# A decoder step on one core: plain 8-block products in place of Strassen's 7 in the first and last part of three token groups

## The chip, the core and the metric

The program runs on one core of one Trainium2 chip. TensorE (PE) multiplies, VectorE (DVE), ScalarE (ACT) and GpSimd (POOL) do the elementwise work, SyncE (SP) issues most weight loads; each engine runs its own instructions in order and waits on semaphores for the others. The metric is device time in microseconds, the lower the better.

## The reference, cut to what matters

One layer of a hybrid decoder over 2048 prompt tokens and 64 sample tokens, in float32. The attention and convolution mixers come first; the change lies in the feed-forward part behind them:

```python
def ffn_sublayer(x, g_pre, w_up_l, w_down_l, g_post):
    h = rmsnorm(x, g_pre)
    a = jax.nn.relu(jnp.einsum('btd,df->btf', h, w_up_l))
    return x + rmsnorm(jnp.einsum('btf,fd->btd', a * a, w_down_l), g_post)
```

with `x` of 2112 x 1024, `w_up` of 1024 x 4096 and `w_down` of 4096 x 1024. The key and value caches of the samples are also copied to outputs, shifted by 8 rows.

## The kernel before

**Number format.** Every float32 operand of a matmul is split in two fp32r tiles: ACT casts it (high part), DVE or POOL subtracts the cast from the original (low part). A product is then three matmuls: high x high, high x low, low x high. A "low" below is such a subtraction, a "split" of weights is a cast and a low.

**Tiling.** The function `out_and_mlp` takes the tokens in four groups (g = 0 to 3) of 512, 512, 512 and 576, and the 4096 hidden columns in eight parts (p = 0 to 7). Part p of group g first makes 4 blocks of 128 hidden columns (`up` steps, i = 0 to 3; 8 blocks of the inner dimension x 3 = 24 matmuls of 512 columns each), ReLU and square on ACT, and then multiplies these 512 hidden columns by the 512 x 1024 block of `w_down` and adds to the group's output `mixed(g)` (tile `em_hx` for even groups, `em_y` for odd ones).

**Strassen.** The product of part p, tokens (2 halves of 256) x hidden (2 halves of 256) times hidden (2) x outputs (2 halves of 512), is done in 7 products (`down` steps in the order P1, P7, P2, P6, P5, P4, P3) instead of 8. Each is 2 token tiles x 2 blocks x 3 = 12 matmuls of 512 columns. The sums of weight blocks lie ready in HBM (`scratch_wt`); the sums of activations are made by DVE (`first_sums`, `second_sums`, `third_sum`: 4 per part), each operand is then split (7 casts on ACT, 5 lows on DVE, 2 on POOL). Two products go to a `shared` tile, which is added to the outputs once per group (`share`: 2 adds of 512 columns, 2 of 1024 in place of four more per part). PE writes products into 5 banks (`y_ps`), DVE adds each to its place (14 additions per part, `add_down`), and PE waits on `y_added` before it takes a bank again.

**Order of work.** `steps()` yields one list, which every engine goes through in the same order. The first two ups of part p + 1 (the *leads*) stand behind P7 and P6 of part p, so that PE has work while operands get ready. In the last part (p = 7) there are no leads; there the `h` steps stand between the products: PE turns the normalised tokens of the next group (8 transposes to two of three `up_ps` banks), ACT casts and DVE takes the low.

Around each unit n, ACT casts the weights of unit n + 2 (it waits for the use of unit n - 1), and DVE or POOL takes their low. DVE does P7, P6 and P3 (in part 7 only P6), POOL all others:

```python
LO_BY_DVE, LO_BY_DVE_LAST = (P7, P6, P3), (P6,)
BY_DVE, BY_POOL = (P1, P7, P2, P6, P5), (P4, P3)
```

Weights are loaded by SP in pieces of 1 MB for two ups or two products, three in flight. The work at the rim of the groups is placed by hand in the tables `POST`, `FIRST`, `ADD`, `PRE`, `SECOND` (norms and residual on the way into the feed-forward part, placed in parts 0 to 2 of group 0 and 5 to 7 of groups 1 and 2) and `END`, `SCALE`, `END_ADD`, `OUT` (final norm, residual and store of group g, placed in part 0 and the start of part 1 of group g + 1):

```python
END_ADD = (("up", 0, 3), ("up", 1, 0), ("up", 1, 0), ("down", 0, P5))
OUT = (("down", 0, P7), ("down", 0, P2), ("down", 0, P6), ("down", 0, P4))
```

`END_ADD` is POOL's `add_residual` (L1977), which waits for the load of the residual `x1` to `ml_res`; `OUT` is ACT's store of a finished tile (`store_y`, which waits for POOL's addition) and its load of the residual two tiles on (L1864). In even parts ACT also issues a copy of 3 MB of the key or value cache from HBM to HBM behind the last up (L118), on the same queue.

Lines: L2095 to L2097 are the matmuls of an up, L2171 those of a product of 7, L2128 those of the mixers' output projection, L2080 the turns of h, L2203 ACT's weight cast, L1983 and L2485 the weight lows of POOL and DVE, L2266 and L2479 cast and low of activations, L2451 their sums, L2511 and L2513 DVE's additions out of the banks, L2534 and L2538 the shares, L2562 a norm's scaling.

## Time and profile before

| what | value |
|---|---|
| time, median of 3 runs | 2646.51 us (2641.0 to 2647.37) |
| the profiled execution: time, span | 2644.41 us, 2642.6 us |
| mean granted TensorE clock | 0.984 |
| PE busy | 2522.6 us, 95% of the span |
| DVE, ACT, POOL busy | 1382.9, 1166.3, 1415.2 us |
| feed-forward parts, roughly | from 1043 us to the end |

A row of the trace names the engine, the line of the kernel, the operation, the tiles written and read with their shapes, and how many instructions it groups. In brackets stands how long the engine was idle before it and what ended that. Times of rows are microseconds from the start of the span. Matmuls overlap: one of 0.39 us starts every 0.23.

### The profile page before, as it was taken

What the parts mean: (1) busy time and instruction counts of PE and PEld (TensorE: products, weight loads), DVE (VectorE), ACT (ScalarE), POOL (GpSimd) and SP (SyncE); (2) the same over time, 40 slices, a digit from 0 to 9 for tenths busy, and PEclk for the clock granted to TensorE, in tenths of its full rate; (3) what the DMA queues carried; (4) which work ended last, traced back from release to release, by engine and by line L of the source; (5) the groups of instructions that cost most, each with busy time, mean ns of one, the idle gap of its engine ahead of it and who ended that gap; (6) DMA issues with size and microseconds to landing.
All of it is one profiled execution on the core that took longest, in us unless ns stands there. A gap on an engine that the chain in (4) does not pass through costs nothing.

```text
span 2642.6 us, 35400 instructions
## 1 busy us (share of the span) xinstructions
PE 2522.6 (95%) x13562; PEld 2167.4 (82%) x13562; DVE 1382.9 (52%) x2231; ACT 1166.3 (44%) x2002; POOL 1415.2 (54%) x818
## 2 busy tenths in 40 slices
PE   7999999999999999999998999998999999999995
PEld 6899999899996468778877788777778778889884
DVE  6431221265663225865566554676555476655657
ACT  4000110187775534545454444554544455444443
POOL 1216560068663566665566675666665475554555
PEclk9999999999999999999999999999999999999998
DMA  5316764299988944564556555456555263553452
GB/s 183 112 44 244 264 230 120 83 164 180 166 146 212 295 160 166 193 208 159 167 183 242 176 168 183 151 170 232 173 173 193 99 235 120 198 178 127 142 191 96
DMA packets 297903, 457.65 MB, mean 173 GB/s; under 512 B 81748, under 2 KB 202140, under 8 KB 290776
## 3 DMA queue, kind: packets, MB, share of 16 engines
q1 hardware_dynamic: 270546, 313.71, 41.3%
q10 hardware_dynamic: 14518, 89.43, 9.5%
q0 software_dynamic: 12672, 52.24, 5.9%
q8 instruction: 109, 1.79, 0.3%
q14 instruction: 58, 0.48, 0.1%
HBM read 390.50 MB, written 120.53 MB: 193 GB/s over the span
## 4 chain that ended last, share of the span: by engine, by line
PE 76%; DVE 10%; DMA 5%; POOL 3%; ACT 3%; issue 2%; SPq 0%; ACTq 0%; DVEq 0%; POOLq 0%
PE ml_y L2171 13%; PE ml_up L2095 8%; PE ml_up L2096 8%; PE ml_up L2097 8%; PE ml_y L2128 6%; PE pj_acc L518 6%; PE pj_acc L519 6%; PE pj_acc L520 6%; PE at_o L1187 5%; PE at_turn L1167 2%; POOL ml_w_lo L1983 2%; DVE ml_a_lo L2479 2%; DVE ml_a_lo_raw L2451 2%; DVE ml_w_lo L2485 2%; PE at_score L1156 2%
## 5 line engine op out<-in xcount | busy, mean ns | idle before, releaser
L1983 POOL TENSOR_TENSOR ml_w_lo<-em_raw,ml_w_hi 128x1024 fp32r<-128x1024 f32 x296 | 741.2, 2512 | 635.1 <-ACT ml_w_hi L2203 634.9
L2203 ACT CAST ml_w_hi<-em_raw 128x1024 fp32r<-128x1024 f32 x384 | 401.4, 1046 | 295.8 <-PE ml_y L2171 189.0
L2095 PE MATMUL ml_up<-ml_h_hi,ml_w_hi 128*128 128x512 f32 (+2 forms) x1280 | 457.1, 357 | 23.3 <-POOL ml_w_lo L1983 23.3
L2096 PE MATMUL ml_up<-ml_h_lo,ml_w_hi 128*128 128x512 f32 (+2 forms) x1280 | 453.5, 354 | 0.0
L2097 PE MATMUL ml_up<-ml_h_hi,ml_w_lo 128*128 128x512 f32 (+2 forms) x1280 | 452.6, 354 | 0.0
L2171 PE MATMUL ml_y<-ml_w_hi,ml_a_hi 128*128 128x512 f32 x896 | 358.2, 400 | 34.4 <-DVE em_hx L2513 13.8
L2171 PE MATMUL ml_y<-ml_w_lo,ml_a_hi 128*128 128x512 f32 x896 | 352.6, 393 | 0.0
L2171 PE MATMUL ml_y<-ml_w_hi,ml_a_lo 128*128 128x512 f32 x896 | 352.3, 393 | 0.0
L2095 PEld LDWEIGHTS ml_up<-ml_h_hi,ml_w_hi 128*128 128x128 f32 x1280 | 243.2, 190 | 66.3 <-POOL ml_w_lo L1983 35.3
L518 PE MATMUL pj_acc<-pj_h_hi,pj_w_hi 128*128 128x424 f32 (+1 forms) x800 | 290.3, 363 | 5.6 <-DVE pj_h_lo L736 5.6
L519 PE MATMUL pj_acc<-pj_h_lo,pj_w_hi 128*128 128x424 f32 (+1 forms) x800 | 283.5, 354 | 0.0
L520 PE MATMUL pj_acc<-pj_h_hi,pj_w_lo 128*128 128x424 f32 (+1 forms) x800 | 283.4, 354 | 0.0
L2485 DVE TENSOR_TENSOR ml_w_lo<-em_raw,ml_w_hi 128x1024 fp32r<-128x1024 f32 x88 | 132.1, 1501 | 264.7 <-ACT ml_w_hi L2203 264.4
L2096 PEld LDWEIGHTS ml_up<-ml_h_lo,ml_w_hi 128*128 128x128 f32 x1280 | 243.4, 190 | 30.7
L2097 PEld LDWEIGHTS ml_up<-ml_h_hi,ml_w_lo 128*128 128x128 f32 x1280 | 243.1, 190 | 31.0
L2171 PEld LDWEIGHTS ml_y<-ml_w_hi,ml_a_hi 128*128 128x128 f32 x896 | 170.1, 190 | 83.8 <-DVE em_hx L2513 15.7
L754 DVE SCALAR_TENSOR_TENSOR pj_proj<-pj_acc,pj_scale,pj_rstd_of 128x424 f32<-128x424 f32 (+1 forms) x100 | 65.0, 656 | 311.0 <-PE pj_acc L520 311.0
L2171 PEld LDWEIGHTS ml_y<-ml_w_hi,ml_a_lo 128*128 128x128 f32 x896 | 170.2, 190 | 36.2
L2171 PEld LDWEIGHTS ml_y<-ml_w_lo,ml_a_hi 128*128 128x128 f32 x896 | 170.5, 190 | 33.6
L2479 DVE TENSOR_TENSOR ml_a_lo<-ml_a_lo_raw,ml_a_hi 128x512 fp32r<-128x512 f32 x128 | 166.9, 1304 | 0.1
L2255 ACT ACTIVATE ml_a<-ml_up 128x512 f32<-128x512 f32 (+1 forms) x80 | 41.0, 513 | 279.4 <-PE ml_up L2097 269.6
L518 PEld LDWEIGHTS pj_acc<-pj_h_hi,pj_w_hi 128*128 128x128 f32 x800 | 150.9, 189 | 15.7 <-issue 8.3
(319 smaller groups left out, 4559.8 us busy)
## 6 DMA issues: line engine op xcount, KB each, us to landing
em_raw<-in_w_up SPq DMA_DIRECT2D x64, 1024.0 KB, 6.2
em_raw<-scratch_wt SPq DMA_DIRECT2D x128, 512.0 KB, 4.7
em_raw<-in_w_down SPq DMA_DIRECT2D x96, 512.0 KB, 3.7
out_o_a_k_s<-in_cache_a_k ACTq DMA_DIRECT2D x8, 3060.0 KB, 11.9
out_o_a_v_s<-in_cache_a_v ACTq DMA_DIRECT2D x8, 3060.0 KB, 13.2
em_raw<-scratch_pt SPq DMA_DIRECT2D x34, 512.0 KB, 7.3
pj_work<-in_w_down POOLq DMA_DIRECT2D x16, 1024.0 KB, 6.3
scratch_wt<-pj_work POOLq DMA_DIRECT2D x16, 1024.0 KB, 4.5
```

The source lines that it names most:

```text
L518: pe.matmul(acc[g][:, 0:n], w_hi[:, i % 2, k, :], h_hi[:, k, cols], start=(k == 0), stop=False)
L519: pe.matmul(acc[g][:, 0:n], w_hi[:, i % 2, k, :], h_lo[:, k, cols], start=False, stop=False)
L520: last = pe.matmul(acc[g][:, 0:n], w_lo[:, i % 2, k, :], h_hi[:, k, cols], start=False, stop=(k == DBLK - 1))
L1983: nc.gpsimd.tensor_tensor(split_of(w_lo, n), raw_of(n), f32(split_of(w_hi, n)), ALU.subtract).then_inc(w_lo_ready, 1)
L2095: pe.matmul(out, hi[:, k, :], h_hi[:, k, cols], start=(k == 0), stop=False)
L2096: pe.matmul(out, hi[:, k, :], h_lo[:, k, cols], start=False, stop=False)
L2097: last = pe.matmul(out, lo[:, k, :], h_hi[:, k, cols], start=False, stop=(k == DBLK - 1))
L2128: last = pe.matmul(out, p[:, f, t0:t0 + m], w[:, b, :], start=(f == 0 and p is act_hi and w is hi), stop=(f == DBLK - 1 and p is act_lo))
L2171: last = pe.matmul(out, p[:, SLOT[i], c:c + P], w[:, f, :], start=(i not in ONTO and f == 0 and p is a_hi and w is hi), stop=(f == DF - 1 ...
L2203: nc.scalar.copy(split_of(w_hi, n), raw_of(n)).then_inc(w_hi_ready, 1)
L2479: nc.vector.tensor_tensor(a_lo[:, slot, :], frm, f32(a_hi[:, slot, 0:2 * HT]), ALU.subtract).then_inc(a_lo_by_dve, 1)
L2485: nc.vector.tensor_tensor(split_of(w_lo, n), raw_of(n), f32(split_of(w_hi, n)), ALU.subtract).then_inc(w_lo_by_dve, 1)
```

## The change

In parts 0 and 7 of groups 0, 1 and 2 (`PLAIN`) the 7 products give way to the plain 8 block products, in four units (`plain` steps, i = 0 to 3): output half i // 2, hidden half i % 2. A unit goes over all 4 token tiles with 2 blocks x 3 matmuls, 24 matmuls of 512 columns; both hidden halves of one output half are accumulated in the same four banks, so that DVE adds 4 times behind units 1 and 3. The other parts, and all of group 3, keep the 7 products.

- Operands: no sums. The two token halves of the first two hidden blocks are cast and lowered at the third up, those of the other two at the fourth (4 casts, 4 lows by DVE).
- Weights: two loads of 1 MB straight from `w_down`; all lows of plain units fall to POOL (`lo_by_dve` holds for `down` steps alone).
- Leads: behind units 0 and 2. h turns in part 7: the first ahead of unit 0, then behind units 0, 1, 2 (two behind unit 2 in group 2, which has a fifth, narrow tile to turn).
- The shares of the `shared` tile move from the start of the next group to the third and fourth up of part 7 of the same group; the final norm of a tile waits for its last plain addition.
- Entries of the tables that name a product of a plain part go to a unit by `IN_PLAIN`: P1 and P7 to unit 0, P2 and P6 to 1, P5 to 2, P4 and P3 to 3.
- Semaphore counts of the operands go by parts of seven (`sevens_before`) and plain parts (`plains_before`).

```diff
+    PLAIN = ((0, LAST), (0, LAST), (0, LAST), ())
+    PLAINS = 2 * DF
+    PLAIN_LEADS = (0, 2)
+    PLAIN_H = {0: (1,), 1: (2,), 2: (3, 4)}
+    PLAIN_SLOT = ((SLOT[P1], SLOT[P7]), (SLOT[P2], SLOT[P4]))
+    IN_PLAIN = {P1: 0, P7: 0, P2: 1, P6: 1, P5: 2, P4: 3, P3: 3}
...
+                if is_plain(g, part):
+                    if part == LAST and g + 1 < NG:
+                        yield "h", g + 1, 0, 0
+                    for i in range(PLAINS):
+                        yield "plain", g, part, i
+                        if part < LAST and i in PLAIN_LEADS:
+                            yield "up", g, part + 1, PLAIN_LEADS.index(i)
+                        for j in PLAIN_H.get(i, ()):
+                            if part == LAST and g + 1 < NG and j < len(tiles(g + 1)):
+                                yield "h", g + 1, 0, j
+                    continue
...
+                if kind == "plain":
+                    half = i // DF
+                    sp.dma_start(to.rearrange("p (k c) -> p k c", c=HALF),
+                                 down_v[part][:, :, half * HALF:(half + 1) * HALF]).then_inc(landed, 16)
+                    return
...
+            def product_plain(n):
+                step = UNITS[n]
+                kind, g, part, i = step
+                half, f0 = divmod(i, DF)
+                wait_lo(pe, n)
+                pe.wait_ge(plain_lo, 4 * plains_before(step) + 2 * (f0 + 1))
+                hi, lo = split_of(w_hi, n), split_of(w_lo, n)
+                for j in range(PROMPT_TILES):
+                    q = sum_at(("plain", g, part, half * DF + DF - 1), j)
+                    if f0 == 0:
+                        pe.wait_ge(y_added, BEFORE[q] + 1)
+                    out, slot = y_ps[BANK[q]][:, :], PLAIN_SLOT[f0][j // PAIRS]
+                    for f in range(DF):
+                        c = f * HT + j % PAIRS * P
+                        for p, w in ((a_hi, hi), (a_hi, lo), (a_lo, hi)):
+                            last = pe.matmul(out, p[:, slot, c:c + P], w[:, f, :], start=(f0 == 0 and f == 0 and p is a_hi and w is hi),
+                                             stop=(f0 == DF - 1 and f == DF - 1 and p is a_lo))
...
-                    act.wait_ge(shared_added, PROMPT_TILES * g + j + 1)
+                    act.wait_ge(y_added, sum_at(("plain", g, LAST, PLAINS - 1), j) + 1)
...
-                        if g and part == 0 and i == 0:
-                            share(g - 1)
-                        if i == DF:
+                        if i == DF and is_plain(g, part):
+                            for q in range(2):
+                                low_plain(step, q + 1, PLAIN_SLOT[0][q], a[:, q, :, :].rearrange("p f t -> p (f t)"))
+                        elif i == DF:
...
+                        if i == PF - 1 and is_plain(g, part):
+                            for q in range(2):
+                                low_plain(step, q + 3, PLAIN_SLOT[1][q], a_raw[:, KEPT + q, :])
+                        elif i == PF - 1:
                             second_sums(step)
+                        if i >= DF and is_plain(g, part) and part == last_of_seven(g) + 1:
+                            share(step)
+                    elif kind == "plain":
+                        if part == last_of_seven(g) + 1 and i == DF - 1:
+                            dve.wait_ge(shared_added, PROMPT_TILES * (g + 1))
+                        for j in sums_of(step):
+                            add_plain(step, j)
```

## Rows read from the trace of the kernel before

**Rows 1.** The page: busy time of each engine, and the chain that ended last
```profile
PE 2522.6 (95%) x13562; PEld 2167.4 (82%) x13562; DVE 1382.9 (52%) x2231; ACT 1166.3 (44%) x2002; POOL 1415.2 (54%) x818
...
PE 76%; DVE 10%; DMA 5%; POOL 3%; ACT 3%; issue 2%; SPq 0%; ACTq 0%; DVEq 0%; POOLq 0%
```

**Rows 2.** PE's waits over the span: total, times, longest
```profile
PE ml_up L2095 <- POOL ml_w_lo L1983: 23.3, 29, 6.1
PE ml_y L2171 <- DVE em_hx L2513: 13.8, 6, 4.5
```

**Rows 3.** Windows of the six parts: length, busy (x instructions), clock, DMA
```profile
1042.66:1099.29 56.63, 54.06 (x229) 43.66 (x228) 34.70 (x34) 32.19 (x50) 34.44 (x14) 0.97 0.58 195
1361.03:1385.94 24.91, 23.23 (x117) 18.94 (x116) 20.95 (x28) 14.98 (x22) 17.44 (x8) 1.00 0.46 148
1385.94:1449.20 63.26, 55.33 (x230) 44.03 (x228) 38.66 (x39) 30.92 (x46) 38.88 (x19) 0.95 0.66 238
1768.83:1794.96 26.13, 23.53 (x118) 18.96 (x116) 22.17 (x28) 14.98 (x22) 17.43 (x8) 1.00 0.44 141
1794.96:1858.73 63.77, 55.41 (x230) 44.09 (x228) 38.66 (x39) 30.89 (x46) 38.84 (x19) 0.95 0.65 235
2188.72:2220.51 31.79, 25.93 (x125) 20.71 (x124) 26.30 (x32) 16.33 (x25) 18.36 (x8) 0.95 0.36 115
```

**Rows 4.** The chain at the out projection of group 2: start, us, what
```profile
1622.98 43.53 PE ml_y L2128 x192
```

**Rows 5.** Timeline of PE, a turn of h: start, us, what
```profile
1378.71 1.04 PE L2080 MATMUL ml_up<-all_ident,em_y 128*128 128x128 f32 x8
1379.51 0.48 PE L2171 MATMUL ml_y<-ml_w_hi,ml_a_hi 128*128 128x512 f32 x1
```

**Rows 6.** The chain in part (1,0)
```profile
1413.04 14.44 DMA ml_res<-scratch_x
...
1427.62 2.34 POOL em_hx L1977
...
1430.29 2.32 POOL ml_w_lo L1983
```

**Rows 7.** Timeline of PE at the second leads of (1,0) and (2,0)
```profile
1432.65 0.79 PE L2095 MATMUL ml_up<-ml_h_hi,ml_w_hi 128*128 128x512 f32 x1 [5.68 <-POOL ml_w_lo L1983]
...
1440.45 0.39 PE L2171 MATMUL ml_y<-ml_w_hi,ml_a_hi 128*128 128x512 f32 x1
...
1842.12 0.80 PE L2095 MATMUL ml_up<-ml_h_hi,ml_w_hi 128*128 128x512 f32 x1 [6.14 <-POOL ml_w_lo L1983]
```

**Rows 8.** Timeline of ACT and its queue in (1,0)
```profile
1410.06 0.58 ACTq L118 DMA_DIRECT2D out_o_a_k_s<-in_cache_a_k  x1
...
1430.43 1.05 ACT L2203 CAST ml_w_hi<-em_raw 128x1024 fp32r<-128x1024 f32 x1 [6.07 <-POOL em_hx L1977]
```

**Rows 9.** Timeline of DVE in (0,0)
```profile
1075.27 3.44 DVE L2485 TENSOR_TENSOR ml_w_lo<-em_raw,ml_w_hi 128x1024 fp32r<-128x1024 f32 x1
...
1078.81 3.22 DVE L2562 SCALAR_TENSOR_TENSOR em_y<-em_y,ml_rstd,ml_gain_post 128x1024 f32<-128x1024 f32 x1
```

**Rows 10.** PE's waits in (2,7), 2188 to 2221
```profile
PE ml_y L2171 <- DVE em_hx L2513: 3.0, 1, 3.0
PE ml_y L2171 <- DVE ml_w_lo L2485: 1.7, 1, 1.7
```

**Rows 11.** Timelines of DVE (wide shares, after groups 2 and 0) and POOL
```profile
2221.53 4.57 DVE L2538 TENSOR_TENSOR em_hx<-em_hx,ml_shared 128x1024 f32<-128x1024 f32 x2
...
2220.92 2.96 POOL L1983 TENSOR_TENSOR ml_w_lo<-em_raw,ml_w_hi 128x1024 fp32r<-128x1024 f32 x1 [0.76 <-ACT ml_w_hi L2203]
...
1390.76 2.35 DVE L2538 TENSOR_TENSOR em_hx<-em_hx,ml_shared 128x1024 f32<-128x1024 f32 x2
```

**Rows 12.** Timeline of ACT in (0,7)
```profile
1362.52 0.63 ACT L2266 CAST ml_a_hi<-ml_a_lo_raw 128x512 fp32r<-128x512 f32 x1
```

**Rows 13.** A window behind PE's wait in (1,0), columns as in rows 3
```profile
1432.00:1436.00 4.00, 3.35 (x8) 2.67 (x9) 0.00 (x0) 0.00 (x0) 4.00 (x3) 0.50 0.50 162
```

More of the change, by code:

```diff
@@ L1497, in out_and_mlp, with is_plain, last_of_seven, first_of_seven @@
     CLOSING_ORDER = (2, 3, 4, 0, 1)
+    PLAIN = ((0, LAST), (0, LAST), (0, LAST), ())
[4 more added lines that the diff above has]
+    IN_PLAIN = {P1: 0, P7: 0, P2: 1, P6: 1, P5: 2, P4: 3, P3: 3}
+    def is_plain(g, part):
+        return part in PLAIN[g]
+    def last_of_seven(g):
+        return max(part for part in range(PARTS) if not is_plain(g, part))
+    def first_of_seven(g):
+        return min(part for part in range(PARTS) if not is_plain(g, part))
+    def sevens_before(step):
+        return sum(not is_plain(*divmod(at, PARTS)) for at in range(step[1] * PARTS + step[2]))
+    def plains_before(step):
+        return step[1] * PARTS + step[2] - sevens_before(step)
     def early_half(j):
@@ L1551, in steps @@
                             yield "conv", g + 1, 0, 0
-                    if part == LAST and g + 1 < NG and i in H_AT[0:len(tiles(g + 1))]:
-                        yield "h", g + 1, 0, H_AT.index(i)
     STEPS = list(steps())
-    UNITS = [step for step in STEPS if step[0] in ("op", "up", "down")]
+    UNITS = [step for step in STEPS if step[0] in ("op", "up", "down", "plain")]
     UNIT_OF = {step: n for n, step in enumerate(UNITS)}
@@ L1571, in sums_of @@
             return list(range(len(tiles(g)))) if i % PD == PD - 1 else []
+        if kind == "plain":
+            return list(range(PROMPT_TILES)) if i % DF == DF - 1 else []
         if kind == "down":
@@ L1581, in out_and_mlp @@
         q += len(sums_of(step))
-        used += step[0] == "op" and not sums_of(step)
+        used += step[0] in ("op", "plain") and not sums_of(step)
     def sum_at(step, j):
@@ L1624, in out_and_mlp, with unit_at @@
     OUT = (("down", 0, P7), ("down", 0, P2), ("down", 0, P6), ("down", 0, P4))
+    def unit_at(kind, g, part, i):
+        if kind == "down" and is_plain(g, part):
+            return "plain", g, part, IN_PLAIN[i]
+        return kind, g, part, i
     def placed(places, late):
@@ L1632, in placed @@
                 first = 0 if g == 1 else LAST - 2
-                found.setdefault((kind, g - 1, first + part, i), []).append((g, j))
+                found.setdefault(unit_at(kind, g - 1, first + part, i), []).append((g, j))
         for j in range(len(tiles(0))):
@@ L1729, in out_and_mlp @@
         shared_added = ph.sem("shared_added")
+        plain_hi = ph.sem("plain_hi")
+        plain_lo = ph.sem("plain_lo")
         lower_ready = ph.sem("lower_ready")
@@ L2179, in _ @@
                     turn_mix(step)
+                elif step[0] == "plain":
+                    product_plain(n)
+                    n += 1
                 elif step[0] == "h":
@@ L2523, in add_down @@
                 elif i in (P1, P6):
-                    add_sum(shared[:, j, :], src, part == 0 and i == P1)
+                    add_sum(shared[:, j, :], src, part == first_of_seven(g) and i == P1)
                 elif i in (P7, P5):
@@ L2530, in add_down, with add_plain @@
                     add_sum(at[:, j, left if i == P2 else right], src, part == 0)
+            def add_plain(step, j):
+                kind, g, part, i = step
+                q, half = sum_at(step, j), i // DF
+                dve.wait_ge(y_done, q + 1)
+                add_sum(mixed(g)[:, j, half * HALF:(half + 1) * HALF], y_ps[BANK[q]][:, :], part == 0)
             def share_right(g, j):
@@ L2538, in share_both, with share @@
                 nc.vector.tensor_tensor(at, at, shared[:, j, :].unsqueeze(1).to_broadcast([P, 2, HALF]), ALU.add).then_inc(shared_added, 1)
-            def share(g):
-                dve.wait_ge(y_added, FIRST_Q[("up", g + 1, 0, 0)])
-                for j in range(PAIRS):
-                    share_right(g, j)
-                for j in range(PAIRS):
-                    share_both(g, j)
+            def share(step):
+                kind, g, part, i = step
+                if i == DF:
+                    dve.wait_ge(y_added, FIRST_Q[step])
+                    for j in range(PAIRS):
+                        share_right(g, j)
+                else:
+                    for j in range(PAIRS):
+                        share_both(g, j)
             def samples_done(late):
@@ L2665, in _ @@
                     if kind == "up":
-                        if g and part == 0 and i == 0:
-                            share(g - 1)
-                        if i == DF:
+                        if i == DF and is_plain(g, part):
+                            for q in range(2):
+                                low_plain(step, q + 1, PLAIN_SLOT[0][q], a[:, q, :, :].rearrange("p f t -> p (f t)"))
+                        elif i == DF:
                             first_sums(step)
```

54 lines of the change are left out of this document (37 added, 17 removed).

## The prediction

> **What bounds the kernel now.** I read the page first: PE is busy for 95% of the span and carries 76% of the chain that ended last, DVE 10%, DMA 5% [rows 1]. So a matmul more costs its whole duration, and other engines count only where PE waits for them. The list of PE's waits says for whom: POOL's and DVE's low halves of weights, and DVE's sums [rows 2]. Next I cut the six changed parts out of the timeline, from their first matmul to that of the next stretch [rows 3], and ask how much of each is idle. I write (g,p) for part p of group g.
>
> The yardstick is PE's pace. 192 matmuls of 512 columns with no wait among them took 43.53 us, 0.2267 each [rows 4]. That stretch is also the nearest relative of the new units: units of 24 matmuls that go over four banks of y with 6 each. Eight transposes and their switch took 0.80 us [rows 5].
>
> Idle before, a stretch less its matmuls and transposes:
> - (0,0): 4 ups, 7 products and the 2 leads and 2 ups up to the next product, 96 + 84 + 48 = 228 matmuls, 51.7 us of 56.6: 4.9.
> - (1,0), (2,0), the same count: 63.3 and 63.8 long, so 11.6 and 12.1.
> - (0,7), (1,7): 84 matmuls and 4 h turns, 19.0 + 3.2 = 22.2 us of 24.9 and 26.1: 2.7 and 3.9.
> - (2,7): 84 matmuls, 4 turns and a narrow fifth (0.6, estimated from the same row), 22.8 of 31.8: 9.0.
>
> Sum 44.2 us [rows 3]. The stalls sit where 12-matmul units (2.7 us) meet norms, turns or late data, and the change replaces just these units.
>
> **What it adds.** A part takes 4 x 24 = 96 matmuls for 7 x 12 = 84. Six parts: 72 x 0.2267 = +16.3 us, all on PE.
>
> **What it removes off PE.** Per part 3 of 11 weight splits on ACT, all DVE weight splits (3, or 1 in part 7), the 4 operand sums, 2 POOL lows; PSUM additions fall from 14 to 8, operand lows from 7 to 4. The weight loads fall from 3.5 to 2 MB. None of this was on PE's path by itself, so I value it only through the idle that stays.
>
> **Part (0,0).** PE waited for DVE: a weight low of 3.44 us and a norm of 3.22 stood ahead of the additions that free the banks [rows 9]. Afterwards the first additions are due 12 us behind the last up, with no split or sum before them, and each bank has over 4 us until it is wanted again (one spare bank, 1.36 us per tile). The norm is still there and is hidden by those 12 us. I leave 0.3: 96 + 96 + 48 = 240 matmuls, 54.4 + 0.3 = 54.7 against 56.6, **-1.9**.
>
> **Parts (1,0), (2,0).** Here the row of causes is long and mostly stays. At the third tile's final residual POOL waits for a load of x1 that took 14.44 us, as it stands on ACT's queue behind the 3 MB cache copy; then POOL adds (2.34), merges, and only then splits the weights of the second lead, for which PE waited 5.7 us until 1432.65 [rows 6 to 8]. The change moves none of these in POOL's order: the addition stays at the first lead, the split behind it. The copy is issued perhaps 0.5 us later (one more cast of 0.6 [rows 12] ahead of it), the load of x1 about 1 us earlier, as ACT no longer waits for DVE's sums; behind the copy that gains nothing. The load for the next ups (1 MB) now falls into the copy, while before 1 MB of products was issued just ahead of it: equal bytes. I add 1 us for it: the second lead starts at 1433.7.
>
> What changes is what PE does meanwhile. It reaches the product at 1385.94 + 96 x 0.2267 = 1407.7 and has 4 units of 24 until the second lead, not 72 matmuls with short waits among them: 21.8 us, so it arrives at 1429.5 and waits 4.2 us, not 5.7. Behind the wait the clock was at its lower level (0.50 of 2.4 GHz) [rows 13], and the unit took 7.80 us for 5.44 [rows 6, 7], 2.4 lost; a shorter wait should lose less, I take 1.5. After the lead only 24 matmuls stand, not 36 with 0.6 us of waits. End: 1433.7 + 5.4 + 1.5 + 5.4 = 1446.0 against 1449.2: **-3.2**. The wait for the first lead's split (1.4 us) goes too, absorbed ahead of the same due time. In (2,0) the second lead starts at 1842.12 [rows 7], 25.4 us behind its first product instead of 25.0, the stretch ends at 1858.7: 1843.1 + 12.3 = 1855.4, **-3.3**.
>
> Now both middle stores of y (tiles 1 and 2) fall on one plain unit. ACT stands at the second until POOL has added, as it did before [rows 8]. Queued behind it is the split for the last unit: ACT at 1431.5-1432.5, POOL free of the lead's split at 1433.7, ready at 1436.1, wanted at 1440. Hidden by 4 us; without cover it would cost its 3.4.
>
> **Parts (x,7).** PE waited for DVE's splits and additions (4.7 us of (2,7) [rows 10]); these go. But two things arrive: the shares, formerly at the next group's start, now lie on DVE in the last two ups, and h turns come earlier. The second turn needs, for its second half, the bank that the first turn filled, so DVE must have taken its lows. From the last up's end (0): ReLU, square and two casts end at 2.7 (the first cast began at 1.5 before [rows 12]), two lows at 3.5, two wide shares of 1.2 each at 5.9 [rows 11], the low half at 6.5. PE has the first turn, a unit and half a turn: 0.8 + 5.4 + 0.4 = 6.6. Just in time. If POOL's split is under way, a wide share took up to 3.4 (4.57 less 1.2) [rows 11], and PE would wait 2.2. I take 1.0, nearer the middle, as POOL's split becomes due at 4.7 to 4.8, just when the second share starts.
> The Trainium skill ("SBUF — State Buffer", Who interferes with whom) says that VectorE with two SBUF inputs and a reading GpSimd instruction exclude one another for a whole instruction. The stretched share agrees; by that rule whoever starts first wins, and the sum would be 3 us lower or 3.6 higher over the three parts.
> With 0.4 for switches, (0,7) becomes 96 x 0.2267 + 3.2 + 1.4 = 26.4 against 24.9, **+1.5**, and (1,7) 26.4 against 26.1, **+0.3**. In (2,7) turns four and five are adjacent: the fifth's second half needs the fourth's first half emptied (a cast and a low, 1.3 us, with 0.6 of PE beside them): 1.0 more with its start. 21.8 + 3.8 + 2.4 = 28.0 against 31.8, **-3.8**.
>
> The other parts, group 3 and the attention stay. The four shares leave the start of groups 1 to 3, where PE waits for nothing.
>
> **Sum.** -1.9 - 3.2 - 3.3 + 1.5 + 0.3 - 3.8 = -10.4 us: +16.3 of matmuls, 26.7 of idle removed. The profiled execution had 2644.4 (span 2642.6), 2.1 below the median of 2646.5. One like it would take 2634.0; the median goes to **2636.1**.
>
> **Bounds.** x1 landing 2 us earlier or 3 later than I say, twice: -4 to +6; the clock behind the wait, 0 to 2.4 for 1.5, twice: -3 to +1.8; the bank of the second turn, 0 to 2.2, three times: -3 to +3.6. Together -10 to +11.4 about -10.4, if all fall alike.
>
> **Rivals.**
> - **The gain is used up, no change (0.22).** The ups' load slows the copy and x1 lands 3 us later than assumed, and every wide share meets a POOL split: -10.4 + 6 + 3.6 = -0.8, 2645.7. For it: the copy's queue already holds x1 for 14 us, and DVE stretches are common. Against: the bytes do not grow.
> - **x1 lands before it is wanted (0.12).** If the copy runs freely once the products' loads are gone, the split is ready at 1429.5: 4.2 + 1.5 go twice, -10.4 - 11.4 = -21.8, 2624.7. For it: fewer bytes late in the part. Against: x1 waits for the copy, which nobody shortens.
> - **Slower (0.06): POOL as the only splitter behind one late load.** All eight weight lows of a part are now POOL's, in order behind the residual. From the second lead on, each us by which x1 lands later is paid once per part. To add 8 us to the median x1 must land 9.2 us later than I say (about 1438) in both; at 1440 it gives -10.4 + 22.8, say 2659. For it: before, DVE split two of the late units past a blocked POOL. Against: nothing in the queue has 9 us to add.
> - The forecast (-16 to -5) keeps 0.60.
>
> Within 0.3% (7.9 us; about what a measurement of this kernel tells from no change) lies 0.12 of the forecast, its weak end, and the first rival: 0.34. Faster: 0.48 + 0.12 = 0.60. Slower: 0.06. The range 2624 to 2648 spans both neighbours and leaves out the slow rival and the tails.
>
> **What would show it.** Right: 72 more matmuls at 0.2267 in the plain units, no PE wait for DVE's splits in the six parts; PE's wait at the second lead of (1,0) and (2,0) about 4 us; (0,0) near 54.7 us, (1,0) near 60, (0,7) near 26.4. Wrong: the second lead starting more than 2 us away from 1433.7 (relative to the part's first matmul), a wait over 2 us in each second turn, waits in parts that I call unchanged, or a lower clock in plain units.

## The result: 22 us faster, twice the forecast

| | before | after |
|---|---|---|
| first comparison, median | 2644.62 us (2641.0 to 2647.37, 4 runs) | 2622.32 us (2618.78 to 2626.2, 4 runs) |
| ratio, 95% interval | | 0.9917 (0.9894 to 0.994) |
| second comparison, median | 2645.2 us (2634.97 to 2652.49, 17 runs) | 2623.9 us (2620.03 to 2627.44, 6 runs) |
| ratio, 95% interval | | 0.9912 (0.9896 to 0.9929) |
| all executions of all comparisons, median | 2643.4 us (68) | 2623.1 us (11) |

The direction was right; the size was not. The forecast was 10.4 us less, the measurement says 20 to 22, and 2622.3 lies just outside the range of 2624 to 2648.

The profiled execution of after took 2619.1 us (span 2617.3). Its page, the lines that answer to [rows 1]:

```profile
PE 2522.5 (96%) x13634; PEld 2174.1 (83%) x13634; DVE 1300.4 (50%) x2153; ACT 1137.7 (43%) x1966; POOL 1381.8 (53%) x800
...
PE 80%; DVE 8%; DMA 4%; POOL 3%; ACT 3%; issue 2%; SPq 1%; ACTq 0%; DVEq 0%; POOLq 0%
```

PE has exactly the 72 matmuls more that the sum counts (13634 against 13562), and yet it is busy for no longer: it lost less to the lower clock. The mean granted clock is 0.990 against 0.984, which over the spans is about 15 us less lost (an estimate from these two figures), nearly the 16.3 us that the matmuls cost. DVE carries 8% of the chain, not 10%.

PE's waits over the span of after, as in [rows 2]:

```profile
PE ml_up L2138 <- POOL ml_w_lo L2026: 12.1, 24, 3.3
PE ml_y L2214 <- DVE em_hx L2602: 9.0, 3, 4.5
```

The wait of the ups for POOL's lows has halved (12.1 us from 23.3), and the longest is 3.3 us where it was 6.1.

Windows of the six parts in after, columns as in [rows 3]:

```profile
1040.15:1094.56 54.41, 54.41 (x242) 45.05 (x241) 17.01 (x20) 27.47 (x44) 31.46 (x12) 1.00 0.56 193
1355.98:1381.33 25.35, 25.35 (x130) 21.40 (x128) 13.35 (x19) 10.36 (x16) 10.52 (x4) 1.00 0.25 84
1381.33:1439.30 57.97, 54.69 (x241) 44.97 (x240) 22.09 (x21) 26.37 (x40) 35.45 (x16) 1.00 0.66 238
1754.18:1779.53 25.35, 25.35 (x129) 21.39 (x128) 13.35 (x19) 10.36 (x16) 10.51 (x4) 1.00 0.25 84
1779.53:1838.51 58.98, 56.29 (x241) 46.16 (x240) 22.23 (x21) 26.37 (x40) 35.71 (x16) 0.97 0.65 234
2167.52:2194.51 26.99, 26.41 (x137) 22.06 (x136) 14.20 (x21) 11.01 (x18) 10.53 (x4) 1.00 0.25 82
```

In the first, second and fourth the busy time of PE equals the length: nothing is idle. The reader is to hold them against the forecast one by one:

| part | before | forecast | after |
|---|---|---|---|
| (0,0) | 56.6 | 54.7 | 54.4 |
| (1,0) | 63.3 | 60.1 | 58.0 |
| (2,0) | 63.8 | 60.5 | 59.0 |
| (0,7) | 24.9 | 26.4 | 25.4 |
| (1,7) | 26.1 | 26.4 | 25.4 |
| (2,7) | 31.8 | 28.0 | 27.0 |
| sum | 266.5 | 256.1 | 249.1 |

All six came out shorter than forecast, by 7.0 us together. That is a pattern, not scatter, and the main finding of this study: nearly all of the allowances that the sum had added were too large. ("Before" is here the one profile that the prediction read; how far one profile can be trusted comes below.)

What stayed of the wait in (1,0), in the chain of after:

```profile
1407.12 15.96 DMA ml_res<-scratch_x
1423.21 2.38 POOL em_hx L2020
1425.93 2.32 POOL ml_w_lo L2026
```

It is the old row of causes [rows 6], link by link: the load of x1 behind the cache copy, POOL's addition, the split, the lead. The second leads of (1,0) and (2,0), from PE's timeline:

```profile
1428.29 0.50 PE L2138 MATMUL ml_up<-ml_h_hi,ml_w_hi 128*128 128x512 f32 x1 [3.28 <-POOL ml_w_lo L2026]
...
1825.90 0.79 PE L2138 MATMUL ml_up<-ml_h_hi,ml_w_hi 128*128 128x512 f32 x1 [2.69 <-POOL ml_w_lo L2026]
```

The first starts 46.96 us behind the first matmul of its part (46.71 before, 47.8 forecast), the second 46.37 (47.16 before, 48.1 forecast). PE waits 3.3 and 2.7 us, not the 4.2 forecast. Read also the durations: 0.50 in the one and 0.79 in the other, which is the lower clock level (the mean clocks of the two windows above are 1.00 and 0.97). The shorter wait was the one that was followed by it.

Part (0,7) of after, DVE, POOL and PE in their timelines:

```profile
1358.12 1.29 DVE L2568 TENSOR_TENSOR ml_a_lo<-ml_a_lo_raw,ml_a_hi 128x512 fp32r<-128x512 f32 x2 [6.90 <-ACT ml_a_hi L2342]
1359.34 2.35 DVE L2633 TENSOR_TENSOR em_hx<-em_hx,ml_shared 128x1024 f32<-128x1024 f32 x2
1361.61 1.28 DVE L2533 TENSOR_TENSOR ml_h_lo<-ml_up,ml_h_hi 128x512 fp32r<-128x512 f32 x2
...
1360.61 3.33 POOL L2026 TENSOR_TENSOR ml_w_lo<-em_raw,ml_w_hi 128x1024 fp32r<-128x1024 f32 x1 [5.14 <-ACT ml_w_hi L2271]
...
1362.32 1.04 PE L2123 MATMUL ml_up<-all_ident,em_y 128*128 128x128 f32 x8
```

POOL's split was due at 1360.61, about 0.1 us behind the start of the second share (1359.34 plus half of 2.35). So the share kept its 1.2 us, and it was the split that took 3.33 instead of 2.40. DVE's first low of h ended at about 1362.3, and PE turned at 1362.32 without a wait.

### The profile page after: what moved, and what is told of

Same layout as the page of the kernel before. It is cut to its first block, busy times and chain, and to the rows that moved or that the text cites. A ratio compares the mean times of both kernels' runs of the same rounds, so it can differ in the third digit from the quotient of the medians.

```text
span 2617.3 us, 35342 instructions
## 1 busy us (share of the span) xinstructions
PE 2522.5 (96%) x13634; PEld 2174.1 (83%) x13634; DVE 1300.4 (50%) x2153; ACT 1137.7 (43%) x1966; POOL 1381.8 (53%) x800
## 4 chain that ended last, share of the span: by engine, by line
PE 80%; DVE 8%; DMA 4%; POOL 3%; ACT 3%; issue 2%; SPq 1%; ACTq 0%; DVEq 0%; POOLq 0%
PE ml_y L2214 12%; PE ml_up L2138 8%; PE ml_up L2140 8%; PE ml_up L2139 8%; PE ml_y L2171 6%; PE pj_acc L518 6%; PE pj_acc L519 6%; PE pj_acc L520 6%; PE at_o L1187 4%; PE ml_y L2234 4%; PE at_turn L1167 2%; POOL ml_w_lo L2026 2%; PE at_score L1156 2%; PE at_score L1157 1%; DVE ml_a_lo L2564 1%
## 5 line engine op out<-in xcount | busy, mean ns | idle before, releaser
L2026 POOL TENSOR_TENSOR ml_w_lo<-em_raw,ml_w_hi 128x1024 fp32r<-128x1024 f32 x290 | 726.1, 2511 | 652.2 <-ACT ml_w_hi L2271 652.1
L2271 ACT CAST ml_w_hi<-em_raw 128x1024 fp32r<-128x1024 f32 x366 | 382.5, 1045 | 312.2 <-PE ml_y L2214 168.8
L2138 PE MATMUL ml_up<-ml_h_hi,ml_w_hi 128*128 128x512 f32 (+2 forms) x1280 | 454.6, 355 | 12.1 <-POOL ml_w_lo L2026 12.1
L2214 PE MATMUL ml_y<-ml_w_hi,ml_a_hi 128*128 128x512 f32 x728 | 287.7, 395 | 22.0 <-DVE em_hx L2602 9.0
L2214 PE MATMUL ml_y<-ml_w_lo,ml_a_hi 128*128 128x512 f32 x728 | 285.1, 392 | 0.0
L2214 PE MATMUL ml_y<-ml_w_hi,ml_a_lo 128*128 128x512 f32 x728 | 285.0, 392 | 0.0
L2574 DVE TENSOR_TENSOR ml_w_lo<-em_raw,ml_w_hi 128x1024 fp32r<-128x1024 f32 x76 | 106.0, 1395 | 222.5 <-ACT ml_w_hi L2271 222.2
L2214 PEld LDWEIGHTS ml_y<-ml_w_hi,ml_a_hi 128*128 128x128 f32 x728 | 137.4, 189 | 58.8 <-DVE em_hx L2602 10.3
L2214 PEld LDWEIGHTS ml_y<-ml_w_hi,ml_a_lo 128*128 128x128 f32 x728 | 137.4, 189 | 29.3
L2214 PEld LDWEIGHTS ml_y<-ml_w_lo,ml_a_hi 128*128 128x128 f32 x728 | 137.6, 189 | 27.6
L520 PEld LDWEIGHTS pj_acc<-pj_h_hi,pj_w_lo 128*128 128x128 f32 x800 | 150.9, 189 | 2.7
## 6 DMA issues: line engine op xcount, KB each, us to landing
out_o_a_v_s<-in_cache_a_v ACTq DMA_DIRECT2D x8, 3060.0 KB, 11.6
```

The lines of the kernel that those rows point to most:

```text
L520: last = pe.matmul(acc[g][:, 0:n], w_lo[:, i % 2, k, :], h_hi[:, k, cols], start=False, stop=(k == DBLK - 1))
L2026: nc.gpsimd.tensor_tensor(split_of(w_lo, n), raw_of(n), f32(split_of(w_hi, n)), ALU.subtract).then_inc(w_lo_ready, 1)
L2138: pe.matmul(out, hi[:, k, :], h_hi[:, k, cols], start=(k == 0), stop=False)
L2214: last = pe.matmul(out, p[:, SLOT[i], c:c + P], w[:, f, :], start=(i not in ONTO and f == 0 and p is a_hi and w is hi), stop=(f == DF - 1 ...
L2271: nc.scalar.copy(split_of(w_hi, n), raw_of(n)).then_inc(w_hi_ready, 1)
L2574: nc.vector.tensor_tensor(split_of(w_lo, n), raw_of(n), f32(split_of(w_hi, n)), ALU.subtract).then_inc(w_lo_by_dve, 1)
```

## The experiments

All ratios are against the kernel before in the same comparison.

| kernel | time, us | ratio (95%) |
|---|---|---|
| first part alone | 2626.58 | 0.9922 (0.9903 to 0.9942) |
| last part alone | 2633.2 | 0.9956 (0.9939 to 0.9973) |
| four quiet parts plain as well | 2639.24 | 0.9998 (0.9985 to 1.0012) |
| after, cache copy later | 2610.22 | 0.9888 (0.9868 to 0.9909) |
| before, cache copy later | 2629.08 | 0.9953 (0.9936 to 0.9971) |
| before, short lows on DVE | 2632.36 | 0.9945 (0.9925 to 0.9965) |
| after, DVE loaded | 2635.97 | 0.998 (0.9959 to 1.0) |
| two more parts plain | 2609.95 | 0.9902 (0.9873 to 0.9931) |
| five more parts plain, copies later | 2602.5 | 0.9841 (0.9813 to 0.9869) |

### How much do two profiles of one kernel differ?

No edit: before was profiled four times more, after twice. What was expected of them:

> The kernel before, as it is, for a second profile. Theory A: the six parts are again 56.6, 24.9, 63.3, 26.1, 63.8 and 31.8 us long to within 1 us, while stretches outside them move by some us, above all the one from (1,1) to (1,7), 319.6 us, down to 315. Rival B: that stretch stays at 319 to 320.

> The kernel before, as it is, for a third profile. If the waits of part 7 fall one of two ways from execution to execution, (0,7), (1,7) and (2,7) are each near 36 to 37 (38.9 in group 2) or near 40.7 (42.7), while (0,3) to (0,6) stay at 41.3 to 0.1 us; and (0,1), (1,5), (1,6) are each 44.2 or 45.8.

> The kernel before, a fourth profile. Three profiles give 299.1, 295.7 and 299.8 us for the six stretches and times of 2636.7 to 2644.4, while the median of its timed runs is 2640 to 2648. Theory H: in a common execution the waits of (0,7) and (1,7) have a longer form too (40.7 us, as the run with plain part 0 alone and the run with the later copy showed one each), and the six stretches come to 303 or more when the time is over 2645. If a time over 2645 comes with stretches below 300, the rest lies outside the changed parts.

> The kernel before, a fifth profile; the same question. Expected: between 295 and 305 us in the six stretches, (0,1), (1,5), (1,6), (2,5) each at 44.2 or 45.8.

> The changed kernel, as it is, timed again. Theory A: the gain lies in the six changed parts, where the two profiles show 17.4 us less; the 8 us less elsewhere come from clock and waits that differ from execution to execution. Then the time is 17 to 19 us (0.65 to 0.7%) below before, and the stretch from part (1,1) to part (1,7), 319.6 us before and 314.9 after, differs from execution to execution. Rival B: the change shortens the unchanged parts too; then the time is 22 to 25 us (0.85 to 0.95%) below before and that stretch is again about 315 us.

> The changed kernel, a third profile. Two profiles give 281.7 and 283.2 us for the six stretches. Theory A: again 281 to 284, with (0,0) 54.4, (0,7) and (1,7) 36.2, (2,7) 37.9 to 0.1 us and only (1,0), (2,0) moving between 58 and 60.

Lengths of the changed parts in microseconds, cut from PE's timelines. Here and below a part runs from its first up that is not a lead to that of the next part, so parts (x,7) hold two ups (10.9 us) that the windows above leave out:

```
         before: 1st 2nd   3rd   4th   5th   mean  | after: 1st 2nd  3rd   mean
(0,0)    56.63 55.14 55.14 55.16 56.79  55.77  | 54.41 54.40 54.40  54.40
(1,0)    63.26 62.82 62.80 63.23 62.75  62.97  | 57.97 59.68 57.84  58.50
(2,0)    63.77 64.79 65.06 65.55 65.75  64.98  | 58.98 58.78 58.76  58.84
(0,7)    35.79 37.04 37.01 39.19 37.08  37.22  | 36.24 36.24 36.24  36.24
(1,7)    37.01 37.03 37.04 39.25 39.24  37.91  | 36.24 36.23 36.24  36.24
(2,7)    42.67 38.86 42.78 38.88 38.88  40.41  | 37.88 37.89 37.88  37.88
six      299.1 295.7 299.8 301.3 300.5  299.3  | 281.7 283.2 281.4  282.1
span     2642.6 2635.0 2636.3 2641.4 2634.3 2637.9 | 2617.3 2621.3 2616.8 2618.5
```

Single parts of before jump between a few lengths. The cause can be read in (0,7), the waits of PE in the fourth and the fifth profile of before:

```profile
PE ml_y L2171 <- DVE em_hx L2513: 2.9, 1, 2.9
PE ml_y L2171 <- DVE ml_w_lo L2485: 1.7, 1, 1.7
```

```profile
PE ml_y L2171 <- DVE ml_w_lo L2485: 1.7, 1, 1.7
PE ml_y L2171 <- DVE em_hx L2513: 0.7, 1, 0.7
```

The same wait, 2.9 us or 0.7, and the part 39.19 or 37.08 long. The timelines of DVE and POOL agree to 0.02 us up to 23.3 us behind the start of the part. There they part. First the fourth profile, then the fifth:

```profile
1369.36 2.88 DVE L2479 TENSOR_TENSOR ml_a_lo<-ml_a_lo_raw,ml_a_hi 128x512 fp32r<-128x512 f32 x1
1369.35 2.35 POOL L1983 TENSOR_TENSOR ml_w_lo<-em_raw,ml_w_hi 128x1024 fp32r<-128x1024 f32 x1
```

```profile
1368.87 0.67 DVE L2479 TENSOR_TENSOR ml_a_lo<-ml_a_lo_raw,ml_a_hi 128x512 fp32r<-128x512 f32 x1
1368.86 2.93 POOL L1983 TENSOR_TENSOR ml_w_lo<-em_raw,ml_w_hi 128x1024 fp32r<-128x1024 f32 x1
```

A low of an operand by DVE and a split of weights by POOL come due within 0.01 us of one another. Either DVE's low takes 0.67 us and POOL's split is stretched to 2.93, or the split takes 2.35 and the low 2.88, and then the additions behind the low come 2.2 us later. This low took 0.7 us in nine of the fifteen parts 7 of the five profiles, all of them 37.0 to 37.1 or 38.9 us long, and 2.88 in five, which are 39.2 or 42.7 long. The fifteenth, the 35.79 of the first profile, left the others earlier. So the distinct lengths are the two outcomes of one near tie.

Yet the sum of the six in the profile that the prediction used, 299.1, is the mean of the five. So the forecast of the six parts as a whole did not fail because its profile was odd. In single parts it was: (2,0) was 63.8 us long there and 65.0 in the mean. The six parts account for 17.2 us (299.3 - 282.1) of the 19.4 between the mean spans. Of the rest 2.0 lie in the other 18 parts of groups 0 to 2 (876.3 against 874.3), where before alone scatters by 5.5, so they can't be called an effect. Of the expectations, that each of the six would repeat within 1 us failed in five of them. The stretch from (1,1) to (1,7) did fall to 315 us in before itself (314.6 in the second profile), so the 5 us less that the first pair of profiles shows there are scatter, as theory A had it; the time is nonetheless 21 to 23 us lower in the second comparison, nearer to rival B's figure. No profile of before took over 2645 us, so theory H could not be tried. The third profile of after came out as expected, to 0.2 us.

### Each part of the change alone

```diff
-    PLAIN = ((0, LAST), (0, LAST), (0, LAST), ())
+    PLAIN = ((0,), (0,), (0,), ())                 # first part alone; turns and shares as before
+    PLAIN = ((LAST,), (LAST,), (LAST,), ())        # last part alone
```

> Only part 0 of groups 0 to 2 takes the plain 8 products; part 7 keeps the 7, with the turns and the shares where they were. Theory A: the stretches (0,0), (1,0), (2,0) change as in the changed kernel, -2.2, -5.3, -4.8, together -12.3 us (0.47%), part 7 stays as before. Rival C, that the gain of part 0 hangs on the shares having left the start of the next group: then (1,0) and (2,0) keep over 2 us more than in the changed kernel, and the total is -8 us or less.

> Only part 7 of groups 0 to 2 takes the plain 8 products, with the shares and turns as in the changed kernel. Theory A: (0,7) +0.4, (1,7) -0.8, (2,7) -4.8 us, together -5.1 us (0.2%), and (1,0), (2,0) as before, with the wait of 5.7 us at the second lead. Rival C: leaving the shares out of the next group's start shortens (1,0) and (2,0) by 2 us each, so -9 us.

By the ratios the first part alone gave 0.78% (20.6 us of 2645.2), the last alone 0.44% (11.6 us); both more than expected. In the profiles the changed parts add up: first alone 54.4, 59.4 and 59.2 in the three parts 0 against the mean 55.8, 63.0 and 65.0 (-10.7 us), last alone 36.2, 36.2 and 37.9 against 37.2, 37.9 and 40.4 (-5.2), together 15.9 of after's 17.2. The times don't add up, 32 us against 22; the median of the first rests on 4 runs, 2621.8 to 2631.2. The intervals allow them to: their weak ends are 0.58% and 0.27%, 22 us together. (1,0) and (2,0) did not keep over 2 us more with the shares where they had been, so the rival of the first run did not occur. That of the second, which gave them 2 us each for the shares having left, is open for one of the two: with the last part alone (1,0) took 63.4 us and (2,0) 63.0, where the five profiles of before have 63.8 to 65.8 for it. The load of x1 took 14.65 us in it there, and 14.9 to 16.6 in before. One profile can't tell whether the moved shares did that.

### Where the units cost their full price

```diff
+    PLAIN = ((0, 2, 3, 4, 5, LAST), (0, LAST), (0, LAST), ())
```

> The changed kernel, and also parts 2 to 5 of group 0 take the plain 8 products. These parts have no norms, turns or late data and 0.2 us of waits each; their stretches are 41.3 us. Theory A: 12 matmuls cost their 2.72 us and the small gap of 0.45 goes, so each of the four stretches becomes 43.5 us, together +9.0 us over the changed kernel. Rival D, that the plain part is faster than its count of matmuls says (less work on DVE and ACT, one switch of bank less): under +6. Rival E, that POOL as the only splitter is near its limit: over +12.

Parts (0,2) to (0,5) have waits of 0.2 us each in after and take 41.3 us. As plain parts they took 43.52 each: 192 matmuls by 0.2267 is 43.53. So the price of plain units is their matmuls alone, and where PE doesn't wait a plain part loses 2.25 us (12 matmuls, 2.72, less some 0.5 of small gaps between the short units). The whole kernel lost more than these 9.0: its span is 17 us over after's mean, which is the figure of rival E, though the price in the four parts is theory A's. The rest lies in parts that the edit does not touch: (1,0), (2,0), (1,2) and (2,6) were longer by 2.4, 1.0, 1.9 and 2.6 in that profile. In (1,0) PE's wait at the second lead was 3.6 us, little more than after's 3.1 to 3.4, but the lower clock behind it cost 2.8 us. Whether the quiet parts have a hand in this is not settled.

### The late load of x1

```diff
-                    if kind == "up" and i == PF - 1 and part % 2 == 0:
+                    if kind == "up" and i == PF - 1 and part in ((1, 2, 4, 6) if g in (1, 2) else (0, 2, 4, 6)):
```

In groups 1 and 2 the copy that stood ahead of x1 is issued in part 1; the same edit in after and in before.

> The changed kernel, with the cache copy of part 0 issued behind the last up of part 1 instead (groups 1 and 2 only). If the wait at the second lead of (1,0) and (2,0) is x1 standing behind the copy, that wait (2.5 to 3.4 us, up to 1.7 of lower clock behind it) goes and both stretches fall to 54.4 us (240 matmuls at 0.2267) from 58 to 59.7: -8 to -10 us against the changed kernel. If x1 is late for another reason (POOL's own order), both stay within 1 us.

> The kernel before with the same move of the copy. (1,0) and (2,0) lose the wait of 5.7 to 6.1 us and the lower clock behind it (2.4) and fall from 63 to 65 us to about 55: -17 us against before. Then the plain products gain nothing in these two parts once the copy is out of the way (54.4 against 55), and most of what they gain there in the changed kernel is cover for the copy. Rival: other waits of the 7 products (bank, weight low) come up behind it and they stay above 58.

Windows of (1,0) and (2,0) of after with the copy later:

```profile
1382.06:1436.46 54.40, 54.40 (x241) 45.05 (x240) 25.03 (x21) 26.29 (x40) 35.79 (x16) 1.00 0.57 196
1776.63:1831.03 54.40, 54.40 (x241) 45.05 (x240) 25.03 (x21) 26.29 (x40) 35.80 (x16) 1.00 0.57 196
```

Both waits are gone: 54.40 is 240 matmuls by 0.2267. In before the same edit left 59.46 and 58.77, and PE's waits in (1,0) are of another kind:

```profile
PE ml_y L2171 <- DVE ml_w_lo L2485: 4.2, 1, 4.2
PE ml_up L2095 <- POOL ml_w_lo L1983: 0.8, 1, 0.8
```

So the four combinations, in microseconds (means of the profiles on the left, one profile each on the right):

| | copy as it was | copy later |
|---|---|---|
| (1,0): 7 products, then plain | 63.0, 58.5 | 59.5, 54.4 |
| (2,0): 7 products, then plain | 65.0, 58.8 | 58.8, 54.4 |

Plain units gain 4.5 and 6.1 with the copy in place and 5.1 and 4.4 without it. So they are worth about as much when x1 is in time. I had expected the 7 products to come close to 55 once the copy was gone; that was wrong. A stall of DVE's weight low had been hidden behind the one of x1, and the plain units remove both it and part of the other.

### DVE's weight lows

```diff
+                few = slice(0, 32 if UNITS[n][1] < NG - 1 and UNITS[n][2] in (0, LAST) else HALF)
+                nc.vector.tensor_tensor(split_of(w_lo, n)[:, :, few], raw_of(n)[:, :, few], f32(split_of(w_hi, n)[:, :, few]), ALU.subtract)
```

Before, with DVE's weight lows in the six parts cut to 32 of 512 columns; the rest of these lows is left out of the result.

> The kernel before, with DVE's weight lows of parts 0 and 7 of groups 0 to 2 cut to 32 of 512 columns a block (the rest of the low half is left out, so the products there lack it). Rival G: without these lows (1.2 to 3.4 us each on DVE) its additions come in time: (0,0) 56.6 to about 52.5, (0,7) and (1,7) 36 to 37 down to 34.5, (2,7) 39 to 43 down to 36, (1,0) and (2,0) 63 to 61; together -12 us, and half of the gain of the change could be had without its matmuls. Theory U: DVE's norms, POOL's hold on shared ports and the 2.7 us units are enough for the waits, and less than 5 us go.

(0,0) fell to 52.66 us, and the parts 7 to 36.03, 36.08 and 37.85, as far as with plain units or further. (1,0) and (2,0) stayed at 62.81 and 64.31. The six are 9.5 us shorter than in the mean of before, for the 12 of rival G and the under 5 of theory U. So DVE's weight lows, and the additions queued behind them, are what PE waited for in (0,0) and in the parts 7; in (1,0) and (2,0) the end is set by x1 as long as the copy is ahead of it. It follows that more than half of the 17.2 us did not need the 72 matmuls. A kernel of 7 products that hands these lows to POOL, and so still computes the result, was not tried.

### Rebuilding the waits on DVE

```diff
-            return kind == "down" and i in (LO_BY_DVE_LAST if part == LAST else LO_BY_DVE)
+            return (kind == "down" and i in (LO_BY_DVE_LAST if part == LAST else LO_BY_DVE)
+                    or kind == "plain" and i in ((1,) if part == LAST else (0, 1, 3)))
...
+                nc.vector.tensor_reduce(idle[:, k:k + 1], frm, AX, ALU.add)
```

After, with weight lows back on DVE and a reduction ahead of each of its operand lows whose result nobody reads.

> The changed kernel, with DVE's work in the six plain parts put back: DVE takes the weight lows of plain units 0, 1 and 3 in part 0 and of unit 1 in part 7 (as many as before), and a reduction over 512 columns that nobody reads stands ahead of each of the 4 operand lows (in place of the 4 sums). Theory U, that units of 24 matmuls (5.4 us) outlast DVE's queue: the six stretches stay as in the changed kernel within 1 us each, no wait of PE over 1 us comes back but that at the second lead, and the time is 0 to 3 us above the changed kernel (ratio 0.991 to 0.992). Rival G, that the waits went because DVE has less to do: waits of 1 to 3 us for DVE come back in part 7 or part 0, and the time is 6 us or more above (0.9935 or more).

(0,0), (1,0) and (2,0) hardly moved: 54.4, 59.8 and 58.4. Parts 7 grew to 40.55, 40.88 and 42.51, and the time is 13 us above the changed kernel's, so for the parts 7 rival G holds. DVE, then POOL, in (0,7):

```profile
1358.72 4.53 DVE L2636 TENSOR_TENSOR em_hx<-em_hx,ml_shared 128x1024 f32<-128x1024 f32 x2
1363.17 1.87 DVE L2534 TENSOR_TENSOR ml_h_lo<-ml_up,ml_h_hi 128x512 fp32r<-128x512 f32 x3
...
1358.81 3.35 POOL L2027 TENSOR_TENSOR ml_w_lo<-em_raw,ml_w_hi 128x1024 fp32r<-128x1024 f32 x1 [11.72 <-ACT ml_w_hi L2272]
```

PE's wait there, and the window behind it:

```profile
PE ml_up L2124 <- DVE ml_h_lo L2534: 2.8, 1, 2.8
```

```profile
1363.00:1366.00 3.00, 2.10 (x7) 1.90 (x8) 2.37 (x5) 0.94 (x2) 0.00 (x0) 0.54 0.02 5
```

This is the wait that the prediction had feared, at its place. Now POOL's split is due 0.1 us behind the start of the *first* share, gets in between the two, and the shares take 4.53 us (2.35 in after). PE stands for 2.8 us at the turn; behind it the granted clock is 0.54, and together this costs the part 4.3. The Trainium skill ("SBUF — State Buffer", Who interferes with whom) lets whoever starts first keep the ports for its whole instruction; both timelines agree to 0.1 us (4.53 is 2.35 and most of a split of 2.40).

For the parts 0 the run says less than was meant. DVE was busy for 19.8 us in (0,0), where after has 17.0 and before 34.7: three weight lows and four short reductions are a small part of what the change took off DVE there, as the additions, sums and operand lows that are gone did not come back, and the weight lows took 1.2 to 1.6 us each, where [rows 9] has 3.44. In (0,7) it was 23.6 us, nearer to the 25.6 to 29.0 of before. So in the parts 0 it is not shown whether the longer units or DVE's lighter queue took the waits away; the change brought both at once.

### More of it

```diff
+    PLAIN = ((0, LAST), (0, LAST), (0, 5, 6, LAST), ())            # two more parts plain
...
+    PLAIN = ((0, 1, LAST), (0, 5, 6, LAST), (0, 5, 6, LAST), ())   # five more parts plain
-                    if kind == "up" and i == PF - 1 and part % 2 == 0:
+                    if kind == "up" and i == PF - 1 and part in ((1, 3, 4, 6) if g in (1, 2) else (0, 2, 4, 6)):
```

> The changed kernel, and also parts 5 and 6 of group 2 take the plain 8 products. Their stretches are 44.2 to 45.8 and 48.2 us with 2.4 and 4.9 us of waits for DVE's additions, behind norms and weight lows. Theory A (units of 24 outlast DVE's norms): both fall to 43.5, together -5 to -7 us against the changed kernel. Rival F (the norms of group 3 themselves and the POOL additions hold PE up): waits stay over 2 us in (2,6) and the sum is 0 or worse.

> What the runs so far point to: the changed kernel, plain also in (0,1), (1,5), (1,6), (2,5) and (2,6), and the copies of parts 0 and 2 of groups 1 and 2 issued a part later. From the stretches: (1,0) and (2,0) -8 to -10 us, (2,5) and (2,6) -7, (0,1), (1,5) and (1,6) -0.7 to -2.3 each, (1,2) and (2,2) -1 to -3 each as the loads of attention parts no longer stand behind a copy; together -19 to -26 us against the changed kernel, so 2597 to 2604 us. If the copies now delay something else (x1 stores and loads of parts 3 and 5), less than -15.

Parts (2,5) and (2,6), in after and then with two more parts plain:

```profile
2062.55:2108.38 45.83, 43.34 (x181) 34.69 (x180) 35.58 (x35) 28.89 (x45) 29.89 (x12) 0.96 0.43 141
2108.38:2156.63 48.25, 43.29 (x181) 34.73 (x180) 36.92 (x36) 25.11 (x38) 33.52 (x14) 0.96 0.69 235
```

```profile
2058.76:2102.30 43.54, 43.54 (x193) 36.03 (x192) 25.60 (x25) 25.62 (x41) 28.34 (x10) 1.00 0.37 125
2102.30:2145.82 43.52, 43.52 (x193) 36.04 (x192) 24.41 (x22) 19.36 (x31) 30.11 (x11) 1.00 0.65 219
```

7.0 us less in these two, as theory A had it. The timed runs can't confirm a step of that size: the ratio is 0.9902 (0.9873 to 0.9931), after's 0.9917 and 0.9912. The last kernel, plain in five parts more than after, in which PE had waited, and with the copies of groups 1 and 2 in parts 1 and 3, took 2602.5 us, ratio 0.9841, below both kernels compared here (its interval ends at 0.9869, after's begins at 0.9894). Its page:

```profile
PE 2522.0 (97%) x13694; PEld 2180.8 (84%) x13694; DVE 1231.8 (48%) x2083; ACT 1115.0 (43%) x1936; POOL 1362.9 (53%) x790
```

60 matmuls more than after, the same busy time, 20 us less. In its profile (0,1), (1,5), (1,6), (2,5) and (2,6) take 43.5 us each, (1,0) and (2,0) 54.4.

## Why the prediction was right in direction and wrong in size

**What held.**
- *A matmul costs its whole duration; 72 more cost 16.3 us.* Shown: 72 more are there, and the four quiet parts give the price with nothing else in them.
- *The stalls sit where 12-matmul units meet late work of DVE, and the plain units remove them.* Shown from both sides: shorter lows in before take (0,0) and the parts 7 to where plain units take them, and none of the six parts of after keeps a wait of PE for DVE above 0.6 us. Which half of the change does it in the parts 0, the longer units or the work taken off DVE, is not shown.
- *x1 behind the copy stays.* Shown: the leads of the first profile start within 0.8 us of where they did, and moving the copy alone takes 4.1 and 4.4 us off after.
- *Only 24 matmuls stand behind the second lead, and PE gets there later.* Both as written.

**What failed is the size of the allowances.** The mechanism was right; two kinds of terms were mis-sized: the landing of x1 in (1,0) and (2,0), and the 1.0 us for the second turn in each part 7. Against the mean of the three profiles of after the forecast of the six parts is 6.7 us too long (256.1 against 249.4: 282.1 less the three pairs of ups), and the terms are:

| term of the sum | forecast | measured in after (three profiles) | too much by |
|---|---|---|---|
| second lead behind the start of (1,0), of (2,0) | 47.8, 48.1 | 46.8 to 47.1, 46.1 to 46.4 | 2.7 |
| lower clock behind the wait, twice | 3.0 | 0.1 or 1.7 in (1,0), 1.7 in (2,0) | 0.4 |
| rest in (0,0) | 0.3 | 0 | 0.3 |
| wait of the second turn, three times | 3.0 | 0 in all nine | 3.0 |
| adjacent turns in (2,7) | 1.0 | 1.0, of it 0.6 a wait of PE | 0 |

The first three make the 3.6 us of the parts 0 (175.3 forecast, 171.7 measured) but for roundings, the turns the 3.1 of the parts 7 (80.8 against 77.7).

The time itself missed by 13.8 us (2636.1 against 2622.3). Of that 6.7 are these terms, 3.5 are not found in the six parts (below), and 3.0 come from the start of the sum: it set out from a median of 2646.5, while the 68 executions of before have a mean of 2643.5. The last 0.5 is after's mean against its first median. From 2643.5 the same sum would have given 2633.1.

*The second turn* is the instructive one. The prediction saw a race (the second share and POOL's split due at the same moment), knew both ends, 0 and 2.2 us, and took 1.0 "nearer the middle". But in so near a tie neither outcome gives 1.0: the wait is nothing or over 2 us. After came out on one side in all nine turns, each time with POOL's split due about 0.14 us behind the start of the second share; with DVE loaded PE waited 2.8 us in all three. The prediction had worked out both sums, 3 us lower and 3.6 higher, and should have carried them as two cases.

*The load of x1.* 1 us was added because 1 MB of weights for the ups now fell into the copy. But the bytes under the copy were about equal, as the same paragraph said. In (1,0) the load took 15.8 to 16.1 us (14.4 to 14.8 before), but was issued 25.8 us behind the start of the part instead of 27.1. The gain by an earlier issue, which I struck out ("behind the copy that gains nothing"), and the loss by the slower load cancel there. In (2,0) they don't: the load was issued just as much earlier and took 15.1 to 15.4 us, and in before 14.9 in the profile that the prediction read and 16.2 to 16.6 in the other four. So that profile had a quick load in (2,0), and against the mean of before's five (48.35) the second lead starts 2.1 us earlier. Why the load got slower in the one part and quicker in the other is open.

**The rivals.** The time is nearest to that of "x1 lands before it is wanted" (2624.7), but its mechanism did not occur: PE still waited 3.3 and 2.7 us for it. It came true only in the kernel with the copy later. The rival on the other side, POOL as the only splitter behind a late load, did not occur either. Nor did the gain get used up: x1 did not land 3 us later, and no wide share in the parts 7 of after was held up by a split.

**The remaining 3.5 us.** The six parts explain 17.2 of the 20.7 us between the means of all executions (2643.5 and 2622.8). 2.0 are the other parts in the profiles, 0.2 what lies before and behind them, and 1.2 the difference between the profiled executions (2639.7 in the mean of before's five, 2620.2 of after's three) and all of them. Within the intervals of the ratios these can be nothing; whether steadier parts also spare their neighbours is open.

## What to carry to other kernels

Where PE is the bound, saving matmuls by shorter units pays where nothing waits, and can cost more than it saves where something does: here 12 matmuls saved are worth 2.25 us in a quiet part, and giving them up was worth 4.4 to 6.1 us in the two busiest and 1.0 to 2.5 us in the other four. Part of that could perhaps be had by taking the late work off the other engine instead, as the run with short lows suggests. When the sum of a change is mostly stalls removed, don't put a small caution on each line: cautions add up in one direction (6.7 us of 17.2 here), and where two instructions come due within 0.1 us of one another, carry both outcomes as cases and not a value between them. And a wait that is removed can uncover another right behind it, so try the edit with and without its neighbour before a stall is put down to one cause.

## What was unexpected in the hardware

- The lower clock behind a wait of PE is not a matter of the wait's length alone: after 3.28 us in (1,0) of the first profile the next matmul took 0.50 and the clock stayed at its upper level, after 2.69 us in (2,0) it took 0.79. In the second profile (1,0) did fall, and the part took 59.68 us for 57.97. In (2,0) it fell in all three profiles, behind waits of 2.5 to 2.7 us, and in (1,0) in one of three, behind 3.1 to 3.4. A fall cost 1.7 us each time in after, and 2.8 in (1,0) of the kernel with four quiet parts plain.
- The order of one DVE and one POOL instruction, 0.1 us apart in the profile of after, decides over a whole instruction (two shares in 2.35 or 4.53 us), and with the wait and the clock behind it over 4.3 us of a part. In before the same kind of tie, 0.01 us apart, falls now this way and now that in executions of one kernel (0.67 or 2.88 us for one low of DVE), and gives the parts 7 their distinct lengths, 37.0 or 39.2 us. In after the 0.14 us of margin were the same in all three profiles, and so was the outcome.
